# First feed-forward round on unnormalised tiles with a bias, and four re-orderings, in a two-model transformer kernel on one core

## What is computed

```
def modulate(h, shift, scale):
    return h * (1.0 + scale[:, None, :]) + shift[:, None, :]
...
    # first_block, x: (1, 512, 1024)
    pl = project(modulate(rmsnorm(x, g_mix[l]), sh1, sc1), w_in[l], w_dec_up[l], b_dec[l])
    pc = project(modulate(rmsnorm(ctx, g_mix[l]), sh1c, sc1c), w_in[l], w_dec_up[l], b_dec[l])
    ...                                                  # gated linear attention, short convolution
    x = x + gt1[:, None, :] * mix_l
    x = x + gt2[:, None, :] * swiglu(modulate(rmsnorm(x, g_ffn[l]), sh2, sc2), w_ffn_in[l], w_ffn_out[l])
    return rmsnorm(x, g_final)
...
def swiglu(h, w_in, w_out):
    a, b = jnp.split(h @ w_in, 2, axis=-1)
    return (jax.nn.silu(a) * b) @ w_out
```

## Time and profile before

| | before |
|---|---|
| timed runs, us | 2209.23, 2209.47, 2209.47 (median 2209.47) |
| profiled execution, us | 2206.51 |
| its span, us | 2204.8 |
| mean granted TensorE clock | 0.991 |
| TensorE busy | 2159.1 us, 98% |
| VectorE / ScalarE / GpSimd busy | 43% / 40% / 41% |
| HBM read, written | 213.42 MB, 2.10 MB |

### The profile page before, as it was taken

How to read it: one execution, slowest core, us unless ns; L and a number is a source line. 1 busy time by engine, 2 the same in 40 slices (tenths; PEclk the granted TensorE clock), 3 DMA queues, 4 the chain that set the end, 5 groups by cost and what they waited for, 6 DMA issues and landing times.

```text
span 2204.8 us, 29834 instructions
## 1 busy us (share of the span) xinstructions
PE 2159.1 (98%) x10891; PEld 1744.5 (79%) x10891; DVE 954.1 (43%) x1405; ACT 870.9 (40%) x1308; POOL 898.1 (41%) x456
## 2 busy tenths in 40 slices
PE   7999999999998999999999999999999999999997
PEld 4887776678886888888878888888888878888886
DVE  3214555553344222213876333212688875333201
ACT  3414454563324222333374333223566654233222
POOL 3322323334453444444665444445333235444442
PEclk9999999999998999999999999999999999999999
DMA  7211212236552222233213223233221123222231
GB/s 301 67 59 67 68 48 76 68 135 216 174 184 89 98 95 95 77 94 119 77 39 115 95 97 99 78 95 118 87 78 57 57 68 105 95 96 96 80 97 69
DMA packets 63665, 216.41 MB, mean 98 GB/s; under 512 B 7088, under 2 KB 8240, under 8 KB 62448
## 3 DMA queue, kind: packets, MB, share of 16 engines
q1 hardware_dynamic: 63600, 215.55, 29.9%
HBM read 213.42 MB, written 2.10 MB: 98 GB/s over the span
## 4 chain that ended last, share of the span: by engine, by line
PE 94%; DVE 2%; issue 2%; ACT 1%; DMA 1%; POOL 0%; SPq 0%; DVEq 0%; ACTq 0%; POOLq 0%
PE ps L509 29%; PE ps L511 28%; PE ps L510 28%; PE ps L771 1%; PE ps L783 1%; PE ps L1028 1%; DMA ada_w<-in_w_ada_first 1%; POOL w_lo L370 0%; PE ps L791 0%; PE ps L942 0%; PE ps L940 0%; PE ps L941 0%; PE ps L726 0%; PE ps L570 0%; PE ps L869 0%
## 5 line engine op out<-in xcount | busy, mean ns | idle before, releaser
L370 POOL TENSOR_TENSOR w_lo<-w_raw,w_hi 128x1024 fp32r<-128x1024 f32 (+2 forms) x376 | 843.0, 2250 | 1193.5 <-ACT w_hi L1159 1193.2
L509 PE MATMUL ps<-h_hi,w_lo 128*128 128x512 f32 x1920 | 760.7, 396 | 8.7 <-DVE h_lo L1961 5.0
L511 PE MATMUL ps<-h_hi,w_hi 128*128 128x512 f32 x1920 | 749.8, 391 | 0.0
L510 PE MATMUL ps<-h_lo,w_hi 128*128 128x512 f32 x1920 | 749.5, 390 | 0.0
L1159 ACT ACTIVATE w_hi<-w_raw 128x1024 fp32r<-128x1024 f32 (+2 forms) x376 | 370.7, 994 | 536.6 <-PE ps L511 531.4
L509 PEld LDWEIGHTS ps<-h_hi,w_lo 128*128 128x128 f32 x1920 | 361.8, 188 | 102.7 <-issue 19.3
L511 PEld LDWEIGHTS ps<-h_hi,w_hi 128*128 128x128 f32 x1920 | 361.6, 188 | 76.5
L510 PEld LDWEIGHTS ps<-h_lo,w_hi 128*128 128x128 f32 x1920 | 362.0, 189 | 73.3 <-issue 1.0
L509 PE MATMUL ps<-gu_hi,w_lo 128*128 128x512 f32 x528 | 205.4, 389 | 0.0
L510 PE MATMUL ps<-gu_lo,w_hi 128*128 128x512 f32 x528 | 205.4, 389 | 0.0
L511 PE MATMUL ps<-gu_hi,w_hi 128*128 128x512 f32 x528 | 205.4, 389 | 0.0
(11 more groups left out here) (362 smaller groups left out, 2365.3 us busy)
## 6 DMA issues: line engine op xcount, KB each, us to landing
w_raw<-in_w_ffn_in SPq DMA_DIRECT2D x132, 512.0 KB, 3.4
w_raw<-in_w_hg SPq DMA_DIRECT2D x40, 512.0 KB, 3.4
w_raw<-in_w_ffn_out SPq DMA_DIRECT2D x48, 384.0 KB, 3.1
w_raw<-in_w_conv_gate SPq DMA_DIRECT2D x32, 512.0 KB, 3.4
w_raw<-in_w_merge SPq DMA_DIRECT2D x32, 512.0 KB, 4.6
ada_w<-in_w_ada SPq DMA_DIRECT2D x32, 512.0 KB, 4.5
w_raw<-in_w_ffn_out SPq DMA_DIRECT2D x48, 320.0 KB, 2.9
w_raw<-in_w_cp SPq DMA_DIRECT2D x20, 512.0 KB, 3.5
```

What stands on the lines that cost most here:

```text
L370: pool.tensor_tensor(w_lo[s][:, 0:n], raw[s][:, 0:n], w_hi[s][:, 0:n].bitcast(F32), ALU.subtract).then_inc(lo_done[s], 1)
L509: pe.matmul(out, wl, hi, start=first, stop=False)
L510: pe.matmul(out, wh, lo, start=False, stop=False)
L511: return pe.matmul(out, wh, hi, start=False, stop=last)
```

## The change

Six edits:

1. *Query copy.* `act_q(act, 0)` stands ahead of the table loads in `act_start`; `lat` asks for one read fewer.
2. *Projections to heads.* `v_turn(6)` stands between `lat(15)` and `context(15)`, `v_turn(7)` behind the first head's `z` products, with its context part in bank 2; the first decay weights are copied before ScalarE waits for the last value unit.
3. *Merge.* `act_hi` of slot 0 ahead of slot 2's, on GpSimd likewise.
4. *First feed-forward round.* It runs on `x * amp2` (`hs_hi`, `hs_lo`, made column by column beside the mix), as `pe_pair`. The result is multiplied by `rstd`, and what the shift adds, `shift @ W`, is a bias for each output channel: `bias_sums` makes it from the raw weights with `shift_pad`, VectorE copies the row, `bias_turn` turns it to a column. SyncE loads round 1 of the weights only after `bias_sums`. Round 1 and those behind it read normalised tiles as before: they are made in two halves inside `hidden(0)`, and round 1 waits for them tile by tile.
5. *Sums of squares* are added at once instead of one column late, in every `dve_resid`; the level masks on GpSimd are made one at a time between units of the first output projection instead of in one piece before the feed-forward part.
6. *End.* The last square is not added to `acc` but goes into a second norm product; the root goes to PSUM (`rstd_ps`) for VectorE and once more to SBUF for GpSimd, which makes tiles 0 and 1; five stores instead of four.

```diff
-                pe.wait_ge(S["qkv_lat_read"], u if u >= 6 else u - 2)
+                pe.wait_ge(S["qkv_lat_read"], u if u >= 6 else u - 3)
...
                 lat(u)
+                if u == 15:
+                    pe_v_turn(pe, 6)
                 context(u)
-                if u > 8:
-                    v_turn(u - 9)
-            v_turn(7)
+                if 8 < u < 15:
+                    pe_v_turn(pe, u - 9)
...
-            for s in (1, 3, 2, 0):
+            for s in (1, 3, 0, 2):
                 pool_lo(pool, s, Q_MERGE + 1)
...
+        def bias_sums(pe):
+
+            pe.wait_ge(S["mod2_ready"], KC + 2)
+            for s in range(4):
+                pe.wait_ge(raw_full[s], 16 * (Q_FFI[0] + 1))
+                for t in range(2):
+                    for j in range(4):
+                        rows, k = slice(32 * j, 32 * j + 32), j + 4 * t
+                        mm = pe.matmul(ps[rows, 5, s * P:(s + 1) * P], shift_pad[:, k, :], raw[s][:, k * P:(k + 1) * P],
+                                       start=(t == 0), stop=(t == 1), skip_group_check=True)
+            mm.then_inc(S["row_sums"], 1)
+
+        def bias_turn(pe):
+
+            pe.wait_ge(S["row_copied"], KC + 1)
+            for s in range(4):
+                mm = pe.matmul(ps[:, 7, s:s + 1], bias_row[:, s * P:(s + 1) * P], pick[:, 0:1], start=True, stop=True,
+                               skip_group_check=True)
+            mm.then_inc(S["row_turned"], 1)
...
-                    if e == 0:
+                    if e == 0 and isinstance(r, int):
+                        act_split(act, 8, mod2[:, 8:16], 4 * p, 4 * p + 4)
+                        act.wait_ge(S[f"ffn_scaled{p}"], 1)
+                        act.activation(sa[p][:, :], ps[:, 2 * p, :], ACT.Silu, bias=bias[:, 2 * p:2 * p + 1])\
+                           .then_inc(S[f"ffn_sa{p}"], 1)
...
+                    if e == 0 and isinstance(r, int):
+                        dve_split(dve, 16, lambda k: amp2[:, k:k + 1], mod2[:, 8:16], 4 * p, 4 * p + 4)
+                        for s in (2 * p, 2 * p + 1):
+                            dve.wait_ge(unit_done[s], q + 1)
+                            dve.tensor_tensor(ps[:, s, :], ps[:, s, :], rstd[:, :], ALU.mult).then_inc(S[f"ffn_scaled{p}"], 1)
...
+            pe.wait_ge(S["norm_acc"], 7 * 7 - 1)
+            pe.matmul(ps[:, 6, :], ones[:, :], acc[:, :], start=True, stop=False)
+            pe.wait_ge(S["norm_sq"], 8 * 8)
+            pe.matmul(ps[:, 6, :], ones[:, :], sq[1][:, :], start=False, stop=True).then_inc(S["norm_stat"], 1)
```

More of the change, by code:

```diff
@@ L167, in build @@
         x_res = at("x_res", [P, KC, T], F32, 108)
+        hs_hi, hs_lo = at("hs_hi", [P, KC, T], F32R, 128), at("hs_lo", [P, KC, T], F32R, 156)
+        shift_pad = at("shift_pad", [P, KC, 32], F32, 124)
+        bias_row = at("bias_row", [P, 4 * P], F32, 126)
+        bias = at("bias", [P, 4], F32, 125.5)
         x = at("x", [P, KC, T], F32, 60)
@@ L359, in _, with store @@
             sp_ffn(sp, 2)
[L360 to L363, removed]
+            def store(k, n):
+                sp.dma_start(dram["out"][:, k:k + n, :], x[:, k:k + n, :]).then_inc(S["out_stored"], 16)
+            for k in (2, 4):
+                sp.wait_ge(S["out_ready"], k)
+                store(k, 2)
+            sp.wait_ge(S["gpsimd_out"], CPC + 2)
+            store(0, 2)
+            for k in (6, 7):
+                sp.wait_ge(S["out_ready"], k - 1)
+                store(k, 1)
+            sp.wait_ge(S["out_stored"], 16 * 5)
         def pool_lo(pool, s, q, n=D):
@@ L522, in pe_unit, with pe_pair @@
             mm.then_inc(unit_done[s], 1)
-        def pe_pair(pe, q, hi, lo, ready, bank_free=None):
+        def pe_pair(pe, q, hi, lo, ready, bank_free=None, after={}):
             def product(s, k):
@@ L1417, in act_resid @@
                 if gain:
-                    act_high(act, n, gain(n))
+                    act_high(act, n, gain(n), out)
                 if not twice:
@@ L1606, in _ @@
             act_merge(act)
-            act_resid(act, 1, Q_MIX, 0, 4, full)
+            act.wait_ge(S["dve_step"], 10)
+            act_resid(act, 1, Q_MIX, 0, 4, full, gain=lambda k: amp2[:, k:k + 1], out=hs_hi)
             act_rms(act, 1)
-            act_split(act, 8, mod2[:, 8:16])
+            act.wait_ge(S["mod1_ready"], 2 * KC + 1)
             act_ffn(act, 0, 2, 8, gain=lambda k: gain_xg[:, k:k + 1], twice=True)
@@ new lines, in dve_resid @@
+            for n in range(KC):
+                r, s = (n, 3) if per_round == 1 else (n // 4, n % 4)
+                dve.wait_ge(unit_done[s], q0 + r + 1)
+                if gate is None:
+                    ins = dve.tensor_tensor(x[:, n, :], ps[:, bank(n), :], source[:, n, :], ALU.add)
+                else:
+                    ins = dve.scalar_tensor_tensor(out=x[:, n, :], in0=ps[:, bank(n), :], scalar=gate[:, n:n + 1],
+                                                   in1=source[:, n, :], op0=ALU.mult, op1=ALU.add)
+                ins.then_inc(S["resid_x"], 1)
+                if gain:
+                    dve_low(dve, n, h_base, gain(n), parts)
+                if n >= 1 and not (last and n == KC - 1):
+                    (dve_sums if twice else dve_sum)(dve, i, n)
@@ L1944, in dve_rstd, with dve_split @@
             dve.wait_ge(S["norm_rstd"], 2 * i + 2)
-        def dve_split(dve, h_base, gain, shift=None):
-            for k in range(KC + 1):
-                if k < KC:
+        def dve_split(dve, h_base, gain, shift, first, last):
+            for k in range(first, last + 1):
+                if k < last:
                     if k >= 2:
```

262 lines of the change are left out of this document (142 added, 120 removed).

## The result

| | before | after |
|---|---|---|
| timed runs beside each other, us | 2206.18 to 2209.47, median 2209.35 | 2185.84 to 2190.17, median 2187.03 |
| profiled execution, us (span) | 2206.51 (2204.8) | 2187.32 (2185.6) |
| mean granted TensorE clock | 0.991 | 0.997 |

The ratio is 0.9905, with a 95% interval of 0.9887 to 0.9922: 22.3 us less in the medians, 19.2 in the two profiled executions.

A forecast was written before the change was run, and what follows sets the result against it. TensorE, busy in 98% of the span, bounds the kernel, so only its waits can be won: 4.05 + 3.65 + 1.5 + 8.1 + 0.8 = 18.1 us off the 2209.5 median gives 2191.4, range 2188.5 to 2196.5.

The forecast's parts named there:

- query copy: Start of lat(4): TensorE's 2.52 us idle and 1.53 of low clock behind the query copies go; gain 4.05 us.
- projections: End of the projections: value transposes and decay weights moved, first unit 2.3 us sooner, 1.36 low clock gone; gain 3.65.
- merge: Start of the merge: slot 0's w_lo ready 3.3 us sooner, TensorE's wait for it goes; gain 1.5 us (0.0 to 1.6).
- joint, without round 1: Mix to first feed-forward round: 13.8 us lost, less 2.3 bias sums and switch, 0.87 norm product, 0.6 bias_turn.
- new wait in round 1: Feed-forward round 1: TensorE waits for late normalised tiles in three short pieces, costing 1.9 us (0 to 4).
- end: End of kernel: logarithm 0.65 us sooner, 0.15 for GpSimd's two tiles; gain 0.8 us (0.5 to 2.0).
- the bias sums: Between mix and first feed-forward round: 64 small passes cost 2.2 us (1.9 to 4.3), plus 0.1 for the switch.
- 2199.5 (joint unchanged): Rival: round 0 still waits for the norm, the joint keeps 10 of its 13.8 us; 2199.5 us, chance 0.05.
- 2230 (lower clock): Rival: bias sums leave TensorE at the lower clock for the rounds behind; 2230 us after two rounds, chance 0.02.
- rival with a smaller gain at the joint: Rival: late sum or bias row, round 1 waiting 4, or slower bias sums cost 2 to 6 us; say 2195, chance 0.20.
- no wait in round 1: Rival: VectorE gets ahead of the second w_lo, tiles in time for round 1; 1.9 less, 2189.5 us, chance 0.20.
- the sum for the norm product: First feed-forward round: sum of squares ready at 669.2, wanted at 671.0, so the norm product doesn't wait.

The follow-up runs named there:

- apart: Kernel after, with GpSimd making the second low half of round 1 (slot 1) only after the last normalised tile; 2187.97 us, ratio to before 0.9910.

## Why the forecast was off

| term | forecast | the two profiles | all profiles |
|---|---|---|---|
| start phase | 0 | -1.4 | 0, varies by 2 |
| query copy | 4.05 | 4.06 | 4.1 four times, 2.7 once |
| projections | 3.65 | 3.7 | 3.5 to 3.7 |
| merge | 1.5 | 1.8 | 1.75 |
| joint, without round 1 | 10.0 | 8.9 | 9.2 |
| new wait in round 1 | -1.9 | -0.1 | -0.1 to -0.2 |
| gap in the recurrence | 0 | 1.5 | chance |
| end | 0.8 | 0.7 | 1.1 |
| sum | 18.1 | 19.2 | 19.3 |

**What was right.** The places and mechanisms of the query copy (where the clock falls in the kernel before), the projections and the merge, to 0.25 us each; that nothing of them is given back later; that round 0 does not wait for the root, that the bias sums go at the rate of small products and leave the clock up (2.09 for them and the switch, forecast 2.3), that the stores run at full rate at the end (406 GB/s, VectorE busy for 0.19 of that microsecond). The rivals of 2199.5 (joint unchanged) and 2230 (lower clock) did not occur. Of the rival with a smaller gain at the joint one part did, the late sum, at 0.83 us instead of 2 to 6.

**The step that failed: the new wait in round 1.** I put it at 1.9 us, and it is 0.1 to 0.2. The chain was right link by link: VectorE's value of tile 4 is held up by the second `w_lo`, as in the earlier trace rows. Its sizes were not. Counted from the start of the norm product, I had the last tile at 696.2 - 671.0 = 25.2 us and TensorE at it at 23.4. Measured are 687.2 - 663.54 = 23.7 for both, so no idle time shows before it: the tile 1.5 earlier, TensorE 0.3 later. The 1.5 come from the spacing. I let each tile follow the one before by 1.52; but the last low half of a set stands right behind the one before it, with no value between, and comes 0.87 later (the two at 685.58 took 1.62). That is 0.65 for each of two sets, and the rest small differences on the way to the first `w_lo`. The rival *no wait in round 1* is what happened, though not by VectorE getting ahead of the low half. apart bears this out: its tiles 4 to 7 come earlier still, and the time stays. The answer stood in the trace of before, at the last two of its eight tiles, where I had read only the first:

```profile
683.74 1.63 DVE L1961 SCALAR_TENSOR_TENSOR h_lo<-nv,mod,h_hi 128x512 fp32r<-128x512 f32 x2
```

**The second: the sum for the norm product.** "It ended at 668.3 before, and one low half now stands ahead of it: 669.2" counted the last column alone. On that axis (8.1 later than after's) it ended at 671.6. Before, a column was two instructions, and the delay that the late `x` had caused was gone by the fifth column: at the last four, VectorE waited for TensorE. Now a column is an addition, a wait for `hs_hi`, a low half and another addition, some of them held up by GpSimd, 4.4 us in all, and the delay lasts to the last one. That is 0.83 of the 1.1 that the joint is short of its term. `bias_turn` took 0.4 more than its 0.6 (with the step behind it), and the bias sums 0.2 less than forecast. VectorE in the trace of before, at the fifth column:

```profile
647.85 0.75 DVE L1917 SCALAR_TENSOR_TENSOR x<-ps,mod,x_res 128x512 f32<-128x512 f32 x1 [0.98 <-PE ps L511]
```

**The base.** I took 18.1 off a median of three runs which was 1.7 above that of 66. With 2207.8 the same sum gives 2189.7. The gain between the medians is 20.1, which is 2.0 more than 18.1: 1.8 for the wait that is not there, 0.3 for the end and 0.25 for the merge, less 0.8 for the joint, make 1.5. The other 0.5 is not shown; it is within what the clock does by chance in one place (1.5). The rival without a wait, on the right base, would have given 2187.8, and 2187.6 was measured; that is partly luck, since the joint's loss and the other gains cancel. The range took the sum's terms into account, but not the scatter of the base.

## What to carry to other kernels

When an engine gets more work per step of a loop, compute how fast it makes up an earlier delay, not only whether it keeps pace: a late load in front of the loop then becomes late at its end. Lay a late load out in the pieces in which it is read. And before a sum of small terms is put against a median, look how far single executions of the same kernel lie apart; here there were 5 us between the fastest and the slowest, and the median of three was 1.7 off that of 66.

## What the runs showed of the hardware

The same idle stretch of TensorE (2.4 us at the query copies, 1.66 us in the recurrence) was followed by the lower clock level in one execution and not in the next, in 4 of 5 and in 4 of 14 profiles. It costs some 1.5 us each time, and a norm product that meets it takes 1.80 to 2.08 instead of 1.13. What decides it is open. And passes of 128 columns with 32-wide weights take 1.95 us in a row of 64 and 3.70 in a row of 128: the second 64 cost 27 ns each.
